# The order in which GpSimd issues the expert gathers: slots of 4 u and 4 v, or of 2 u, 2 v, 2 u, 2 v

## What is computed

```python
def block(args):            # 128 tokens
    hx, ex, gx = args
    a = jnp.einsum('phkd,pd->phk', u_table[ex], hx)
    act = jax.nn.gelu(a, approximate=False) * gx
    return jnp.einsum('phk,phkd->pd', act, v_table[ex])
```

## Time and profile before

| | us |
|---|---|
| median of three runs | 3263.31 (3259.97 to 3265.36) |
| the profiled execution | 3256.8 |
| its span | 3255.0 |
| GpSimd busy | 2248.7 (69%) |
| TensorE busy | 2169.3 (67%) |
| VectorE busy | 2135.8 (66%) |
| ScalarE busy | 376.8 (12%) |

### The profile page before, as it was taken

How to read it: one execution, slowest core, us unless ns; L and a number is a source line. 1 busy time by engine, 2 the same in 40 slices (tenths; PEclk the granted TensorE clock), 3 DMA queues, 4 the chain that set the end, 5 groups by cost and what they waited for, 6 DMA issues and landing times.

```text
span 3255.0 us, 30844 instructions
## 1 busy us (share of the span) xinstructions
PE 2169.3 (67%) x9895; PEld 968.0 (30%) x9895; DVE 2135.8 (66%) x4892; ACT 376.8 (12%) x807; POOL 2248.7 (69%) x2225
## 2 busy tenths in 40 slices
PE   6886996765766468997856477767455455455566
PEld 5674441212434113453211144334111111111111
DVE  1678766666788855666575657877876665677531
ACT  2212231100110110222100100000100000000000
POOL 0135777767777777777777777777777777777575
PEclk9997997877988779999877688888666767776679
DMA  8479999999999999999999999999999999999998
GB/s 292 178 272 345 355 376 391 390 397 395 404 396 381 355 399 404 401 407 395 384 407 397 377 404 383 393 375 383 355 409 409 410 409 409 409 410 400 362 409 324
DMA packets 361984, 1233.01 MB, mean 379 GB/s; under 512 B 36791, under 2 KB 39247, under 8 KB 361807
## 3 DMA queue, kind: packets, MB, share of 16 engines
q0 software_dynamic: 304352, 1107.83, 87.3%
q1 hardware_dynamic: 35295, 79.16, 6.8%
q10 hardware_dynamic: 22176, 44.04, 3.6%
HBM read 1218.21 MB, written 13.28 MB: 378 GB/s over the span
## 4 chain that ended last, share of the span: by engine, by line
POOL 32%; DMA 29%; PE 21%; issue 11%; DVE 5%; ACT 1%; DVEq 1%; SPq 0%; POOLq 0%; ACTq 0%
DMA v_ring<-in_v_table_dram,eidt 18%; POOL u_ring L847 13%; POOL v_ring L876 13%; PE bank L1853 10%; DMA u_ring<-in_u_table_dram,eid 7%; PE bank L1664 3%; PE bank L1681 2%; PE bank L1739 2%; PE bank L1763 2%; POOL wring L847 2%; DMA wring<-in_u_table_dram,eid 2%; DVE u_ring L1459 1%; POOL xr L876 1%; DMA mixt<-in_v_table_dram,eidt 1%; POOL keyt L876 1%
## 5 line engine op out<-in xcount | busy, mean ns | idle before, releaser
L1853 PE MATMUL bank<-v_ring,act_x 128*32 128x512 f32 x3504 | 987.7, 788 | 724.4 <-DMA v_ring<-in_v_table_dram,eidt 686.8
L847 POOL DMA_INDIRECT u_ring<-in_u_table_dram,eid x888 | 987.9, 1112 | 395.8 <-issue 260.4
L1459 DVE CUSTOM_DVE_ANT_0 u_ring<-u_ring,h 128x1024 f32<-128x1024 f32 x762 | 919.1, 1225 | 503.7 <-DMA u_ring<-in_u_table_dram,eid 485.0
L876 POOL DMA_INDIRECT v_ring<-in_v_table_dram,eidt x876 | 913.4, 1043 | 345.8 <-issue 213.2
L1853 PEld LDWEIGHTS bank<-v_ring,act_x 128*32 128x32 f32 x3504 | 227.8, 133 | 1389.7 <-issue 1379.2
L1763 PEld LDWEIGHTS bank<-hbuf,wring 128*128 128x128 f32 x1984 | 229.8, 195 | 21.3 <-issue 21.3
L1763 PE MATMUL bank<-hbuf,wring 128*128 128x128 f32 (+1 forms) x1984 | 235.8, 280 | 0.0
L1459 DVE CUSTOM_DVE_ANT_0 u_ring<-u_ring,bank 128x1024 f32<-128x1024 f32 x144 | 175.5, 1221 | 87.8 <-DMA u_ring<-in_u_table_dram,eid 66.3
L1681 PE MATMUL bank<-zc,dring 128*128 128x384 f32 x496 | 191.6, 510 | 4.0 <-ACT dring L905 4.0
L1459 DVE CUSTOM_DVE_ANT_0 wring<-wring,bank 128x1024 f32<-128x1024 f32 x96 | 116.7, 1221 | 78.1 <-DMA wring<-in_u_table_dram,eid 64.8
L1853 PE MATMUL bank<-gt,act_x 128*32 128x512 f32 x104 | 85.4, 972 | 116.8 <-DMA mixt<-in_v_table_dram,eidt 116.8
(11 more groups left out here) (294 smaller groups left out, 2239.2 us busy)
## 6 DMA issues: line engine op xcount, KB each, us to landing
wring<-in_w_out_dram ACTq DMA_DIRECT2D x16, 1024.0 KB, 11.7
wring<-in_w_query_dram ACTq DMA_DIRECT2D x16, 1024.0 KB, 11.7
u_ring<-in_u_table_dram,eid POOLq DMA_INDIRECT x888
v_ring<-in_v_table_dram,eidt POOLq DMA_INDIRECT x876, 7.8
wring<-in_w_in_dram ACTq DMA_DIRECT2D x10, 1024.0 KB, 11.6
xr<-in_x_prompt_dram SPq DMA_DIRECT2D x16, 512.0 KB, 7.4
v_ring<-in_w_ada_dram SPq DMA_DIRECT2D x7, 1024.0 KB, 13.6
wring<-in_w_ada_dram SPq DMA_DIRECT2D x5, 1024.0 KB, 9.8
```

The costliest lines, as they stand in the source:

```text
L847: pool.indirect_dma_start(place, None, u_table[0], bass.IndirectOffsetOnAxis(ap=col, axis=0)).then_inc(landed, 16)
L876: pool.indirect_dma_start(place, None, v_table[0], bass.IndirectOffsetOnAxis(ap=eidt[:, b % RING, t:t + 1], axis=0)).then_inc(landed, 16)
L1459: dve.tensor_tensor_reduce(row, row, h2[:, b % 2] if b < IN_PSUM else h2_bank[b][:, :], 1.0, 0.0, ALU.mult, ALU.add, dot[:, b % 2, k:k + 1 ...
L1853: last = pe.matmul(acc[b][h][j * S:(j + 1) * S, :], act_x[:, i % 2, j, a:a + S], v_place(n)[0][:, h * HALF:(h + 1) * HALF], start=(c == 0) ...
```

## The change

In a slot GpSimd issues two u gathers, two v gathers, two u gathers, two v gathers. Nothing else is altered; each call keeps its own waits.

```diff
             for p in range(NB + 1):
                 for c in range(NCH):
-                    for j in range(CH):
+                    for j in (0, 2):
                         if p < NB or c < NSG:
                             u_fetch(p, c * CH + j)
-                    if v_chunk(p * NCH + c):
-                        b, vc = v_chunk(p * NCH + c)
-                        for j in range(CH):
+                            u_fetch(p, c * CH + j + 1)
+                        if v_chunk(p * NCH + c):
+                            b, vc = v_chunk(p * NCH + c)
                             v_fetch(b, vc * CH + j)
+                            v_fetch(b, vc * CH + j + 1)
             for i in range(S):
                 v_fetch(NB, i)
```

## The result

The changed kernel takes 3285.99 us (median of six runs, 3276.65 to 3295.72), the kernel before 3264.98 in the six beside it (3259.97 to 3273.98): ratio 1.0064, 95% interval 1.0046 to 1.0083. It is 21 us slower; I had forecast 24 us faster. A repetition gave 1.0065. Its profiled execution is the slowest of the six (3295.72 us, span 3293.7), that of before lay 8 us under its median. So single profiles are 39 us apart where medians are 21, and where a few microseconds matter I use several profiles of one order.

A forecast was written before the change was run, and what follows sets the result against it. No compute engine was full; GpSimd's gathers, issue and waits were taken to make up the first stage. Terms -15 - 5 - 9 + 2.5 + 2.6 = -24 us gave 3233, as a median 3240 us (own range 3220 to 3255).

The forecast's parts named there:

- Step 1: First stage: GpSimd's waits for v buffers shrink, with two more positions from v1 to the next v2; -15 us.
- Step 2: First stage: GpSimd's four waits for u buffers shrink if VectorE itself ends no later; -5 us, ends -10 and 0.
- Step 3: First stage: gathers are held less by VectorE's dots, which run in pairs, not fours; -9 us, ends -60 and +50.
- B: Rival: slower, landings lock to issues, first-stage gather surplus rises from 211 to above some 260 us; 3298 us, chance 0.20.
- Step 4: VectorE ends its slot 2.48 us later; TensorE waits for the accumulator at the first block's end; +2.5 us.
- Step 5: Last u block: two v gathers, not four, lie behind its row before GpSimd's fold_ready wait; +2.6 us of DMA idle.
- A: Rival: the waits shrink and nothing follows; 3268 us, or 3263 if half of one gain is kept; chance 0.17.
- C: Rival: slower by VectorE's later slot end at all half-blocks, +40 us with half of the gains; 3290 us, chance 0.06.

The follow-up runs named there:

- split_pairs: The changed kernel with VectorE's steps, weigh and finish moved between the slot's first two and last two dots: 3267.75 us, ratio 1.001 to the kernel before.
- stage2_only: The kernel before with pairs from slot 186 on alone: 3269.16 us, ratio 1.0014 to the kernel before.
- split_fours: The kernel before (four u, four v) with VectorE's steps moved between its two pairs of dots: 3259.66 us, ratio 0.9982; repeated, 3260.47 us, 0.9989.
- alternate: The kernel before with single rows in turn, u0 v0 u1 v1 u2 v2 u3 v3, in slots 17 to 247: 3340.98 us, ratio 1.0251.
- lead6_22: The changed kernel with the u gathers issued two rows earlier, still in pairs: 3484.18 us, ratio 1.0036 to the kernel before, which took 3473.3 us there.

## Why the prediction was wrong

**Step 1, waits for v buffers (-15).** Its mechanism was right and its sum wrong. I counted the waits of the third v above 0.35 us, less 0.30 each, by what had ended TensorE's last idle time ahead of them, with the same rule in all traces. A landing of v, with none of TensorE's own steps since: 30 waits of 31.9 us before (32 and 33 in the prediction), 4 of 7.8 after, 2 of 1.8 in the repetition. The two more positions did cover most of them. But the rest of the third v's waits, TensorE at its own steps or behind VectorE, went from 34.6 us to 74.3 (70.0 in the repetition). "The other waits (34 us beyond the 0.30) follow TensorE's mixer steps, which begin after v3, position 7 in both orders: 0" is the sentence that failed: those steps need VectorE's results too, and these come later. Relieved of one wait, GpSimd only came sooner to the next.

**Step 2, waits for u buffers (-5).** Wrong in sign: 14.5 us became 27.4, +7.0 in the account. The condition stood in the step ("if VectorE itself ends no later") and I then priced it as if it held. VectorE ends later, so its dots free the buffers later; at slot 81 the wait went from 4.84 to 6.16 us.

**Step 3, holds (-9).** Right as far as can be told: -9.3 in the account, in a spread of 12 us inside one order, and B's threshold was not neared: 1467.85 - 1343 x 0.94 = 205 us of surplus in the first stage, where B needed 260. By the Trainium skill's rule on the shared port pair ("SBUF — State Buffer", "SBUF: two separate sides"), read as in the prediction, this term would have been 0, since the number of dots is the same. The trace says otherwise when dots are broken up: in split_pairs, with the same dots, the holds are 163 us against 208. The hold depends on where in a dot a start falls. About as many gathers start inside a dot (622 in split_pairs, 593 in the change), but few of them at its very start (holds of full length: 23 against 71): in a run of four, a held gather and its 0.30 us end where the next dot but one begins, as step 3 says, and a run of two has no such dot.

**Step 4, VectorE two positions late (+2.5, ends 0 and +40).** This is the mis-sized term. The named waits of GpSimd behind VectorE's lateness, at slots 50, 114, 146 and 185, rose by 3.7 + 4.4 + 5.7 + 4.0 = 18 us in the profile of the change (15 in the repetition, where slot 50 has 1.1). TensorE waits 19 to 21 us more for VectorE. Slot 18 rose by 6.1 us besides (7.4 in the repetition), of which 2.5 is the order itself and about 3 the later weight tiles of that execution. I had looked for waits that were visible before, and found one. But work that just fits has no wait: slot 114 had none and got 4.65 us. "Mixer steps that TensorE takes from VectorE are laid out one or more slots apart (10 us), which covers 2.5 us" was taken from the planner's gaps and not from when the steps ran, and slot 18 was not considered at all, though its 6.6 us stood in the rows.

**Step 5, the last u block (+2.6).** Right: 21.45 to 23.95 us, +2.5, and the rate in the affected 40 us fell from 312 to 295 GB/s. stage2_only measured 5.5 us for the whole second stage, which contains it.

**The rivals.** B (landings lock to issues) gave 3298 for a reason that the trace rules out. A gave 3263 to 3268 and has its part of truth, since the relieved waits came back. C, slower by step 4, gave 3290 and 0.06, and is what happened; it also had step 2's and step 3's halves in it, so its time is partly luck. My forecast's last sentence, that a shorter wait without a shorter stage would show the reasoning from GpSimd's account wrong, did not come to the test: the waits did not get shorter. The splits put it to the test: 48 us of holds went, and 9 to 29 us of time. GpSimd's sum equals the stage by construction, and a term taken out of it is not thereby taken out of the stage. One estimate of rival B was low: it put a dot some 5 us behind the issue of its row, which is near the least in the first stage (5.2); the median is 8.3 us before and 9.4 in the change.

**Settled and open.** Shown: the loss is in waits; the slots around the block ends and slot 18 have about half of it by themselves; and at the block ends the chain is in the trace, from VectorE's late dot through finish and TensorE's start to GpSimd's third v. With VectorE's steps fitted to them the pairs are level with the kernel before, but not with fours that have the same edit: 8 us stay (split_pairs against split_fours), and some 4 with slots 17 and 18 and those from 187 on spared, at the edge of the noise. Inferred: that the spread half is mostly VectorE's delay; TensorE's longer busy time is the other candidate, and the split changed the holds too. Open: why alternate loses four times as much, and why slots 104 to 111, where no buffer is waited for, took 89.1 us (89.2 in the repetition) instead of 82.7 to 85.7 with more holds (9.5 us against 3.1 to 6.0). Other slots without waits give that back.

## What to carry to other kernels

When the order of issue changes, follow each consumer that takes its inputs in program order: the time at which its last input arrives sets everything behind it in its program, not the buffer that the new order frees sooner. Price a delay of such an engine at every place where another waits for it, those with no wait now among them, since they may have no slack. And a sum over the busiest engine says where its time is, not what a saving brings: count on waits next in line taking back a good part of any saving (here 40 to 80%) until a run shows otherwise.

## What the runs showed of the hardware

A gather that starts inside a dot is held, by an amount that the start fixes: all 220 gathers of before, among the 1344, that start 0.10 to 0.95 us into a dot end 0.80 to 0.82 us behind its end, and so do all 211 of the change. Those that start in the dot's last 0.1 us last 0.93 to 0.95 us and are not held. A running gather does not hold a dot: the dots of the first stage have a mean of 1225 ns before and of 1224 in split_fours, with 49 us less of holds, and the longest of the change is 1296. The Trainium skill ("SBUF — State Buffer", "SBUF: two separate sides") has, for a VectorE instruction with two SBUF inputs such as the dot, the later of the two engines' instructions blocked; the trace shows only the gather's side. The hold is not special to dots: in split_fours a gather that starts 0.31 us into a 1.82 us step of VectorE (line 1268, at 361.30) lasts 2.32 us, to 0.8 us behind the step's end, as behind a dot.

```profile
361.30 1.82 DVE L1268 TENSOR_TENSOR mixt<-zp 128x1592 f32<-128x1592 f32 x1 [2.14 <-ACT zp L934]
361.61 2.32 POOL L847 DMA_INDIRECT u_ring<-in_u_table_dram,eid  x1 [0.31 <-issue]
```

The same kernel took 3265 us in most groups of runs and 3473 us in one; the cause is open. In that group the rate was lower in the second stage too, where the earlier trace rows and the change have 407 to 408 GB/s and a DMA share above one (355 to 364 GB/s in the four kernels of the group). For lead6_22:

```profile
2360.00:3040.00 680.00, 347.84 (x1157) 87.91 (x1158) 411.64 (x923) 40.86 (x72) 453.28 (x460) 0.73 0.94 358
```

The ratio of one edit may differ between the two, and I set none of one group beside one of the other.
